# Five feed-forward layers on one core: up and down chunks interleaved, and up chunks as seven products

## The chip, the cores and the metric

The kernel runs on one core of a Trainium2 chip. The metric is the device time of one execution in microseconds; the kernel before has a median of 2759.59 us over three executions (2759.25 to 2760.49).

## What is computed

A block with token mixers and a cross-attention, followed by layers of a second kind, on 512 tokens of width 1024 in float32. Five times in it stands a feed-forward layer with a hidden width of 2816 (22 tiles of 128). They are called FFN 0 to FFN 4 here; FFN 0 has a convolution of width 3 on its gate, the others are plain:

```
def conv_ffn(n, w_up, conv_w, conv_b, w_down):      # FFN 0
    u, g = jnp.split(n @ w_up, 2, axis=-1)
    gc = sum(gp[:, j:j + S] * conv_w[j] for j in range(CONV_WIDTH)) + conv_b
    return (jax.nn.silu(gc) * u) @ w_down

def swiglu(x, w_gate, w_up, w_down):                # FFN 1 to 4
    return (jax.nn.silu(x @ w_gate) * (x @ w_up)) @ w_down
```

Before each stands an RMS norm, whose gain is folded into the operand x and whose factor 1/rms (`rstd`, one number per token) multiplies the products behind the matmuls. Between FFN 0 and FFN 1 there are two norms in a row (`renorm`).

## The kernel before

**Chunks.** All weights come as one stream of chunks of 128x2048 float32 (1 MB). SP loads each into one of two `stage` slots; ACT rounds it into `w_hi` (fp32r, `split_hi`, L508), DVE writes the rest `w_lo = stage - w_hi` (`split_lo`, L1002), and PE multiplies hi*hi, hi*lo and lo*hi (`products`, L1995 to L1997). `stage`, `w_hi` and `w_lo` have two slots each, so the split of chunk c+2 can start only when PE is done with chunk c, and PE starts chunk c+2 only when its `w_lo` is written (`lo_ready`). A slot of `stage` is loaded anew when its `w_lo` is written.

**A chunk on PE.** A gate or up chunk of eight products gives two hidden tiles of 128x512: 16 weight tiles by 3, so 48 matmuls of 128x512. A gate chunk of seven products (`seven_products`) gives the same two tiles with seven block products in place of eight, on half the tokens each: 7 x 4 x 3 = 84 matmuls of 128x256. For it DVE forms four sums of weight blocks (`gate_sums`, four operations of 128x512 into `s_f`, L1023 to L1028), which are split too (ACT `s_hi`, L517; DVE `s_lo`, L1012), and once per FFN sums of token blocks (`token_sums`, sixteen operations of 128x256 into `t_f`, L1066 to L1071, split into `t_hi` and `t_lo`). The block products are put together by DVE (`gate_early`, `gate_evac`). Gate chunks 4 to 10 of FFN 0 and 2 to 10 of the others are of this kind, 43 in all; all up chunks are of eight products.

**An FFN.** Eleven steps `it`, each with a gate chunk and an up chunk. They stand in three parts of 4, 4 and 3 steps; behind each part four down chunks add into the residual `h`. A chunk's results go from PSUM into `gate_b` or `up_b` (DVE, times `rstd`: L1051, L1059, L1140), ACT applies silu (L579; in FFN 0 behind the convolution, six DVE operations L1126 to L1130), POOL multiplies both (L1873), ACT and DVE split the product into `f_hi` (L561) and `f_lo` (L1150), and the down chunks read it. PSUM is used four banks at a time, in turn.

**Start of an FFN.** PE works on gate chunk 0 while POOL ends the sum of squares; then a matmul with ones (`stat`, L2035), ACT's square root (L531), and DVE's reciprocal (L1080; between FFN 0 and 1 L2040, L843 and L1619) give `rstd`, without which nothing of the FFN leaves PSUM. PE goes on with up chunk 0 meanwhile. The order on DVE is written out by hand (`ffn` in the block of DVE); the place that matters most here is

```
                        gate_evac(i, it)
                        if it + 1 < end:
                            gate_lo(i, it + 1)
```

with the token sums behind it, at step 0 for FFN 1 to 4 and at steps 0 and 1, two groups each, for FFN 0.

Of the kernel before, what the change touches and what calls it, by code (L numbers as in the profile page):

```python
# [51 lines left out]
PARTS = [("a", 0, 4), ("b", 4, 4), ("c", 8, 3)]  # L52
SEVEN_FROM = [4, 2, 2, 2, 2]
NONE_OF = FT // 2


def _down_name(i, part):

    return f"down{i}" if part == "c" else f"down{i}{part}"
# [2795 lines left out]
```

## Time and profile before

| | us |
|---|---|
| median of three executions | 2759.59 |
| the profiled execution | 2758.85 |
| its span, first to last instruction | 2757.0 |
| PE busy | 2736.3 (99%) |
| DVE busy | 1827.6 (66%) |
| ACT busy | 963.3 (35%) |
| POOL busy | 530.6 (19%) |
| DMA engines, mean share in the queue of the weights | 27.5% |

Times are from one profiled execution; a row of a timeline begins with the start and the duration of an instruction. Matmuls overlap, so what one costs is the distance between starts, not its duration. Where a row groups several instructions (x2), the duration is from the start of the first to the end of the last.

### The profile page before, as it was taken

The numbers are of one execution on the slowest core, as the hardware profiler recorded it, in microseconds if no ns is written. First come the engines' busy times: TensorE is split into PE (matmuls) and PEld (weight loads), VectorE is DVE, ScalarE is ACT, GpSimd is POOL, SyncE is SP. The second block draws the span as 40 slices with busy tenths as digits, with TensorE's granted clock in tenths as the row PEclk, the third lists the DMA queues.
The fourth block names the chain that finished last, engine by engine and source line by source line (L and its number), as shares of the span: only waits on it lengthen the run. The fifth ranks groups of instructions, "written<-read, shape, count | busy, mean of one in ns | idle before, by whom it ended". The sixth has DMA issues, their size and how long they took to land.

```text
span 2757.0 us, 35919 instructions
## 1 busy us (share of the span) xinstructions
PE 2736.3 (99%) x14384; PEld 2340.8 (85%) x14384; DVE 1827.6 (66%) x2088; ACT 963.3 (35%) x1122; POOL 530.6 (19%) x364
## 2 busy tenths in 40 slices
PE   9999999999999999999999999999999999999999
PEld 7978889878888888988778889888898888888987
DVE  5778766558586885756575857568475665684754
ACT  4433533443232442323363423234232322242322
POOL 0124014041010452002223200023000142510100
PEclk9999999999999999999999999999999999999999
DMA  4212034223222323232302222322323233222232
GB/s 169 90 62 80 31 107 138 92 77 103 96 96 104 108 91 103 96 107 99 108 31 77 92 99 101 104 98 105 107 92 107 93 107 106 92 94 105 92 107 92
DMA packets 39748, 266.02 MB, mean 96 GB/s; under 512 B 4528, under 2 KB 5808, under 8 KB 8240
## 3 DMA queue, kind: packets, MB, share of 16 engines
q1 hardware_dynamic: 38016, 259.02, 27.5%
q10 hardware_dynamic: 1584, 4.87, 0.5%
q8 instruction: 113, 1.85, 0.3%
q14 instruction: 35, 0.29, 0.0%
HBM read 261.77 MB, written 2.10 MB: 96 GB/s over the span
## 4 chain that ended last, share of the span: by engine, by line
PE 95%; DVE 2%; ACT 1%; issue 1%; POOL 1%; DVEq 0%; POOLq 0%; ACTq 0%
PE ps L1995 30%; PE ps L1997 29%; PE ps L1996 29%; PE ps L2202 1%; DVE w_lo L1002 1%; PE ps L2268 1%; PE ps L2299 1%; ACT w_hi L508 1%; PE ps L2590 1%; PE ps L2562 1%; PE ps L2224 1%; PE ps L2282 0%; PE ps L2574 0%; PE ps L2035 0%; POOL up_b L1857 0%
## 5 line engine op out<-in xcount | busy, mean ns | idle before, releaser
L508 ACT ACTIVATE w_hi<-stage 128x2048 fp32r<-128x2048 f32 x241 | 443.5, 1840 | 1323.3 <-PE ps L1997 1321.1
L1995 PE MATMUL ps<-x_hi,w_hi 128*128 128x512 f32 (+1 forms) x2056 | 775.0, 377 | 0.0
L1996 PE MATMUL ps<-x_lo,w_hi 128*128 128x512 f32 (+1 forms) x2056 | 764.8, 372 | 0.0
L1997 PE MATMUL ps<-x_hi,w_lo 128*128 128x512 f32 (+1 forms) x2056 | 764.2, 372 | 0.0
L1002 DVE TENSOR_TENSOR w_lo<-stage,w_hi 128x2048 fp32r<-128x2048 f32 x241 | 580.8, 2410 | 103.1 <-ACT w_hi L508 103.1
L1995 PEld LDWEIGHTS ps<-x_hi,w_hi 128*128 128x128 f32 x2056 | 388.0, 189 | 69.6 <-issue 4.1
L1996 PEld LDWEIGHTS ps<-x_lo,w_hi 128*128 128x128 f32 x2056 | 388.2, 189 | 69.1 <-issue 3.9
L1997 PEld LDWEIGHTS ps<-x_hi,w_lo 128*128 128x128 f32 x2056 | 387.7, 189 | 68.0
L1873 POOL TENSOR_TENSOR up_b<-up_b,gate_b 128x512 f32<-128x512 f32 x110 | 132.1, 1222 | 1405.0 <-DVE up_b L1140 1405.0
L1995 PE MATMUL ps<-f_hi,w_hi 128*128 128x512 f32 x880 | 343.0, 390 | 2.2 <-DVE f_lo L1150 2.2
L1996 PE MATMUL ps<-f_lo,w_hi 128*128 128x512 f32 x880 | 342.5, 389 | 0.0
L1997 PE MATMUL ps<-f_hi,w_lo 128*128 128x512 f32 x880 | 342.3, 389 | 0.0
L1140 DVE TENSOR_TENSOR up_b<-ps,rstd 128x512 f32<-128x512 f32 x110 | 70.8, 686 | 198.6 <-PE ps L1997 198.5
L1995 PEld LDWEIGHTS ps<-f_hi,w_hi 128*128 128x128 f32 x880 | 165.2, 188 | 38.4 <-DVE f_lo L1150 4.3
L1997 PEld LDWEIGHTS ps<-f_hi,w_lo 128*128 128x128 f32 x880 | 165.2, 188 | 34.5
L1996 PEld LDWEIGHTS ps<-f_lo,w_hi 128*128 128x128 f32 x880 | 165.2, 188 | 34.1
L1164 DVE SCALAR_TENSOR_TENSOR h<-ps,h 128x512 f32<-128x512 f32 x80 | 51.5, 686 | 201.0 <-PE ps L1997 201.0
L1851 POOL TENSOR_TENSOR ssum<-ssum,sq 128x512 f32<-128x512 f32 x64 | 146.4, 2287 | 5.0
L1995 PE MATMUL ps<-t_hi,s_hi 128*128 128x256 f32 x516 | 146.0, 283 | 0.0
L1996 PE MATMUL ps<-t_lo,s_hi 128*128 128x256 f32 x516 | 146.0, 283 | 0.0
L1997 PE MATMUL ps<-t_hi,s_lo 128*128 128x256 f32 x516 | 146.0, 283 | 0.0
L1849 POOL TENSOR_TENSOR sq<-h 128x512 f32 x64 | 77.9, 1217 | 269.5 <-DVE h L1093 263.6
(441 smaller groups left out, 4102.6 us busy)
## 6 DMA issues: line engine op xcount, KB each, us to landing
stage<-in_stream SPq DMA_DIRECT2D x242, 1024.0 KB, 4.8
h<-in_x ACTq DMA_DIRECT2D x2, 1024.0 KB, 5.2
out_x<-h SPq DMA_DIRECT2D x8, 256.0 KB, 2.1
h<-in_x SPq DMA_DIRECT2D x6, 256.0 KB, 3.7
mem_raw<-in_mem ACTq DMA_DIRECT2D x1, 1024.0 KB, 4.7
stage<-in_stream SPq DMA_DIRECT2D x6, 128.0 KB, 4.5
h<-in_x SPq DMA_DIRECT2D x1, 512.0 KB, 5.3
mask_f<-in_constants ACTq DMA_DIRECT2D x1, 448.0 KB, 6.1
```

The costliest lines, as they stand in the source:

```text
L508: act.activation(w_hi[slot][:, 0:width], stage[slot][:, 0:width], ACT.Copy).then_inc(hi_ready, 1)
L1002: dve.tensor_tensor(w_lo[slot][:, 0:width], stage[slot][:, 0:width], w_hi[slot][:, 0:width].bitcast(F32), ALU.subtract).then_inc(lo_ready, 1)
L1140: dve.tensor_tensor(up_b[:, e, :], ps[:, (t + 2 + e) % 4, :], rstd[:, :], ALU.mult).then_inc(acc_evac, 1)
L1164: dve.scalar_tensor_tensor(h[:, m, :], ps[:, (t + m) % 4, :], scale, h[:, m, :], ALU.mult, ALU.add).then_inc(acc_evac, 1)
L1849: pool.tensor_tensor(sq[:, :], row(h, m), row(h, m), ALU.mult).then_inc(sq_ready, 1)
L1851: pool.tensor_tensor(ssum[:, :], ssum[:, :], sq[:, :], ALU.add).then_inc(ss_ready, 1)
L1873: pool.tensor_tensor(up_b[:, e, :], up_b[:, e, :], gate_b[:, e, 1:1 + S], ALU.mult).then_inc(prod_ready, 1)
L1995: pe.matmul(out_ap, wh, xh, start=first, stop=False)
L1996: pe.matmul(out_ap, wh, xl, start=False, stop=False)
L1997: return pe.matmul(out_ap, wl, xh, start=False, stop=last)
L2202: mm = pe.matmul(ps[:, bank, b * P:(b + 1) * P], lhs, rhs, start=True, stop=True)
L2224: mm = pe.matmul(ps[:, 5 + 2 * e, :], QQ[e][:, 0, b * P:(b + 1) * P], A[e][:, b, :], start=(b == 0), stop=(b == BLK - 1))
```

## The change

The parts a, b and c are gone. Each FFN has an order of positions p (`ORDER`): gate 0, up 0, gate 1, up 1, gate 2, up 2, down 0, gate 3, up 3, down 1 and so on to gate 10, up 10, then a tail of four down chunks. One of the eight down chunks in between covers four hidden tiles and one half of the outputs (16 weight tiles, 48 matmuls of 128x512, four banks); the tail covers the last six hidden tiles, as part c did. Even positions use the upper, odd ones the lower part of PSUM, so that PE may begin a chunk when the one two positions ahead of it is out of PSUM.

In FFN 1 to 4 the up chunks 2 to 9 are computed with seven products too, and in FFN 0 gate chunk 3 is: 76 chunks in place of 43. `s_f`, `s_hi` and `s_lo` are still there once; a gate chunk now begins with the products that read the sums (`s_used`), and an up chunk ends with them. The block products are put together in five DVE operations behind the chunk's end (`evacuated`), over wider operands, and silu, the product, `f_hi` and `f_lo` take both tiles in one instruction, except at the last step. The tail's chunks are split over 1536 columns where they hold no more.

The core of the diff (the block of DVE first):

```
-PARTS = [("a", 0, 4), ("b", 4, 4), ("c", 8, 3)]
-SEVEN_FROM = [4, 2, 2, 2, 2]
-NONE_OF = FT // 2
...
+def _order():
+
+    out = []
+    for it in range(STEPS):
+        out += [("gate", it), ("up", it)]
+        if 2 <= it < STEPS - 1:
+            out.append(("down", it - 2))
...
+SEVENS = [{"gate": range(3, STEPS), "up": range(0)}] + 4 * [{"gate": range(2, STEPS), "up": range(2, STEPS - 1)}]
...
+        def two_banks(p):
+
+            return 6 if p % 2 == 0 else 0
+
+        def four_banks(p):
+
+            return 4 * (p % 2 == 0)
...
-        T_GROUPS = {i: {0: [0, 1], 1: [2, 3]} if i == 0 else {0: [0, 1, 2, 3]} for i in range(5)}
-        T_ROUND_AT = {i: 1 if i == 0 else 0 for i in range(5)}
+        T_SUMS = [{0: [0, 1], 2: [2, 3]}] + 4 * [{0: [0, 1, 2, 3]}]
+        T_ROUND = [3, 1, 1, 1, 1]
...
+                if kind == "gate":
+                    act.wait_ge(chunk_done, c - 1)
+                elif (i, p - 1) in S_FIRST:
+                    act.wait_ge(s_used, S_FIRST[i, p - 1] + 1)
                 act.activation(s_hi[:, :], s_f[:, :], ACT.Copy).then_inc(s_rounded, 1)
...
+                if kind == "gate":
+                    split_hi((c, 0), SINGLES)
...
+                dve.wait_ge(first_copied, n + 1)
+                dve.tensor_tensor(blocks[:, 0:2, :], product(2, adjacent), free(first, 0, twice_dims), ALU.add).then_inc(blocks_sum, 1)
...
-                dve.scalar_tensor_tensor(t_f[:, T1, j, :], b11, gain[0], t_f[:, T3, j, :], ALU.mult, ALU.subtract).then_inc(t_sum, 1)
-                dve.scalar_tensor_tensor(t_f[:, T3, j, :], b22, gain[1], t_f[:, T3, j, :], ALU.mult, ALU.subtract).then_inc(t_sum, 1)
+                dve.scalar_tensor_tensor(t_f[:, T1, j, :], b12, gain[0], t_f[:, T3, j, :], ALU.mult, ALU.subtract).then_inc(t_sum, 1)
                 dve.wait_ge(t_sum, done + 1)
-                dve.scalar_tensor_tensor(t_f[:, T2, j, :], b22, gain[1], t_f[:, T1, j, :], ALU.mult, ALU.add).then_inc(t_sum, 1)
-                dve.wait_ge(t_sum, done + 3)
+                dve.scalar_tensor_tensor(t_f[:, T2, j, :], b22, gain[1], t_f[:, T1, j, :], ALU.mult, ALU.subtract).then_inc(t_sum, 1)
+                dve.wait_ge(t_sum, done + 2)
+                dve.tensor_tensor(t_f[:, T3, j, :], t_f[:, T2, j, :], t_f[:, T3, j, :], ALU.subtract).then_inc(t_sum, 1)
                 dve.scalar_tensor_tensor(t_f[:, T4, j, :], b21, gain[1], t_f[:, T2, j, :], ALU.mult, ALU.subtract).then_inc(t_sum, 1)
...
-                for part, base, count in PARTS:
-                    end = base + count
-                    for it in range(base, end):
-                        c, t = gate_chunk(i, it)
-                        gate_evac(i, it)
-                        if it + 1 < end:
-                            gate_lo(i, it + 1)
...
+                for p, (kind, it) in enumerate(ORDER):
+                    c, t = chunk_at(i, p)
+                    f, k = FT * i + 2 * it, 2 * it % 8
+                    dve.wait_ge(chunk_done, c + 1)
+                    if kind == "down":
+                        b, m = four_banks(p), 4 * (it % 2)
...
+                        dve.scalar_tensor_tensor(h[:, m:m + 4, :], ps[:, b:b + 4, :], scale, h[:, m:m + 4, :], ALU.mult, ALU.add).then_inc(acc_evac, 4)
+                    elif kind == "gate":
+                        evacuated(i, p, gate_b[:, :, 1:1 + S])
...
-                        for j in T_GROUPS[i].get(it, []):
+                            dve.wait_ge(f_ready, past(f))
+                            convolved(it)
+                        for j in T_SUMS[i].get(p, []):
                             token_sums(i, j)
...
+                            dve.wait_ge(f_hi_ready, f + e + 1)
+                            dve.tensor_tensor(f_lo[:, k + e, :], up_b[:, e, :], f_hi[:, k + e, :].bitcast(F32), ALU.subtract).then_inc(f_ready, 1)
+                    if kind_at(i, p + 2) == ("up", True):
+                        weight_sums(i, p + 2)
+                    ffn_lo(i, p + 2)
+                    if p == T_ROUND[i]:
+                        token_lo(i, 0)
+                        token_lo(i, 1)
+                    if p == T_ROUND[i] + 1:
+                        token_lo(i, 2)
+                        token_lo(i, 3)
+                    if kind_at(i, p + 3) == ("gate", True):
+                        weight_sums(i, p + 3)
+                    if kind == "up" and it < STEPS - 1:
+                        dve.wait_ge(f_hi_ready, f + 2)
+                        dve.tensor_tensor(f_lo[:, k:k + 2, :], up_b[:, :, :], f_hi[:, k:k + 2, :].bitcast(F32), ALU.subtract).then_inc(f_ready, 2)
...
+                def with_sums():
+                    pe.wait_ge(s_ready, n + 1)
+                    product(6, summed(S2), token_sum(T2))
+                    product(7, summed(S3), token_sum(T3))
+                    product(5, summed(S1), token_sum(T1))
+                    return product(3, summed(S4), tokens(1, 1))
+
+                clear(i, p)
+                pe.wait_ge(t_ready, 4 * (i + 1))
+                if kind == "gate":
+                    with_sums().then_inc(s_used, 1)
                 product(1, single(0, 0), tokens(0, 0))
-                product(2, single(1, 0), tokens(1, 0)).then_inc(seven_done, 1)
-                pe.wait_ge(s_ready, n + 1)
-                pe.wait_ge(t_ready, 4 * (i + 1))
-                product(6, summed(S2), token_sum(T2)).then_inc(seven_done, 1)
-                product(7, summed(S3), token_sum(T3)).then_inc(seven_done, 1)
-                product(5, summed(S1), token_sum(T1)).then_inc(seven_done, 1)
-                product(3, summed(S4), tokens(1, 1))
-                product(4, single(1, 1), token_sum(T4)).then_inc(chunk_done, 1)
+                product(2, single(1, 0), tokens(1, 0)).then_inc(first_done, 1)
+                mm = product(4, single(1, 1), token_sum(T4))
+                if kind == "up":
+                    mm = with_sums()
+                mm.then_inc(chunk_done, 1)
...
+                for p, (kind, it) in enumerate(ORDER):
+                    c, t = chunk_at(i, p)
+                    if kind == "down":
+                        clear(i, p)
+                        for k in range(4):
+                            pe.wait_ge(f_ready, past(FT * i + 4 * (it // 2) + k + 1))
+                            for m in range(4):
+                                mm = products(ps[:, four_banks(p) + m, :], w_at(c, (4 * k + m) * P, P),
+                                              (f_hi[:, 4 * (it // 2) % 8 + k, :], f_lo[:, 4 * (it // 2) % 8 + k, :]), k == 0, k == 3)
                         mm.then_inc(chunk_done, 1)
```

On DVE, the order of a step p is now: results of chunk p, then the token sums (position 0; FFN 0: 0 and 2), then the sums and splits of the weights of chunk p+2, then weight sums of a gate chunk at p+3, then `f_lo`.

DVE at the start of FFN 2, from the reciprocal on. Before (`w_lo_57` is the slot that gate chunk 1 uses):

```order
L1080 RECIPROCAL rstd<-ssum 128x512
L1051 TENSOR_TENSOR gate_b<-ps,rstd 128x512 x2
L1002 TENSOR_TENSOR w_lo_57<-stage_53,w_hi_55 128x2048
L1066 SCALAR_TENSOR_TENSOR t_f<-h,par,t_f 128x256
L1067 SCALAR_TENSOR_TENSOR t_f<-h,par,t_f 128x256
L1069 SCALAR_TENSOR_TENSOR t_f<-h,par,t_f 128x256
L1071 SCALAR_TENSOR_TENSOR t_f<-h,par,t_f 128x256
```

And in the change:

```order
L1104 RECIPROCAL rstd<-ssum 128x512
L1065 TENSOR_TENSOR gate_b<-ps,rstd 128x2x512
L1090 SCALAR_TENSOR_TENSOR t_f<-h,par,t_f 128x256
L1092 SCALAR_TENSOR_TENSOR t_f<-h,par,t_f 128x256
L1094 TENSOR_TENSOR t_f<-t_f 128x256
L1095 SCALAR_TENSOR_TENSOR t_f<-h,par,t_f 128x256
...
L1024 TENSOR_TENSOR w_lo_57<-stage_53,w_hi_55 128x2048
L1065 TENSOR_TENSOR up_b<-ps,rstd 128x1024
```

The split of gate chunk 1 stood ahead of the sixteen token sums and now stands behind them (the four rows of `t_f` come four times in both; of the change three times four are left out).

DVE in FFN 2, from the end of an up chunk of seven products to the end of the down chunk behind it, in the change:

```order
L1083 TENSOR_TENSOR up_b<-blocks,rstd 128x1024
L1037 TENSOR_TENSOR s_lo<-s_f,s_hi 128x2048
L1024 TENSOR_TENSOR w_lo_56<-stage_52,w_hi_54 128x1536
L1194 TENSOR_TENSOR f_lo<-up_b,f_hi 128x1024
L1159 SCALAR_TENSOR_TENSOR h<-ps,h 128x2048
L1050 TENSOR_TENSOR s_f<-stage_53 128x512
L1051 TENSOR_TENSOR s_f<-stage_53 128x512
L1053 TENSOR_TENSOR s_f<-s_f,stage_53 128x512
L1055 TENSOR_TENSOR s_f<-stage_53,s_f 128x512
L1024 TENSOR_TENSOR w_lo_57<-stage_53,w_hi_55 128x1536
L1037 TENSOR_TENSOR s_lo<-s_f,s_hi 128x2048
```

Each chunk of seven products brings four `s_f`, one `s_lo` and one `w_lo` of 1536 columns, and this now happens for gate and up in each group of gate, up and down.

DVE at the end of an FFN, behind the results of the last gate chunk, in the change:

```order
L1024 TENSOR_TENSOR w_lo_57<-stage_53,w_hi_55 128x1536
L1177 TENSOR_TENSOR up_b<-ps,rstd 128x512 x2
L1180 TENSOR_TENSOR f_lo<-up_b,f_hi 128x512 x2
L1024 TENSOR_TENSOR w_lo_56<-stage_52,w_hi_54 128x1536
```

Before, a `w_lo` of 2048 columns stood between `up_b` and `f_lo` there.

## Rows read from the trace of the kernel before

**Rows 1.** The page, parts 1 and 2:
```profile
PE 2736.3 (99%) x14384; PEld 2340.8 (85%) x14384; DVE 1827.6 (66%) x2088; ACT 963.3 (35%) x1122; POOL 530.6 (19%) x364
...
PEclk9999999999999999999999999999999999999999
```

**Rows 2.** Timeline of PE, two chunks of FFN 0 (start, duration, instruction):
```profile
756.55 0.28 PE L1995 MATMUL ps<-x_hi,w_hi 128*128 128x256 f32 x1
...
766.62 0.40 PE L1995 MATMUL ps<-x_hi,w_hi 128*128 128x512 f32 x1
...
777.53 0.28 PE L1995 MATMUL ps<-x_hi,w_hi 128*128 128x256 f32 x1
```

**Rows 3.** Timeline of PE, start of FFN 2:
```profile
1528.39 0.79 PE L1995 MATMUL ps<-x_hi,w_hi 128*128 128x512 f32 x1
...
1539.68 0.39 PE L1995 MATMUL ps<-x_hi,w_hi 128*128 128x512 f32 x1
```

**Rows 4.** Timeline of DVE, start of FFN 2:
```profile
1529.71 3.35 DVE L1080 RECIPROCAL rstd<-ssum 128x512 f32<-128x512 f32 x1 [5.05 <-ACT ssum L531]
1533.10 1.29 DVE L1051 TENSOR_TENSOR gate_b<-ps,rstd 128x512 f32<-128x512 f32 x2
1534.30 2.28 DVE L1002 TENSOR_TENSOR w_lo<-stage,w_hi 128x2048 fp32r<-128x2048 f32 x1
1536.50 0.48 DVE L1066 SCALAR_TENSOR_TENSOR t_f<-h,par,t_f 128x256 f32<-128x256 f32 x1
1536.90 0.48 DVE L1067 SCALAR_TENSOR_TENSOR t_f<-h,par,t_f 128x256 f32<-128x256 f32 x1
1537.29 0.48 DVE L1069 SCALAR_TENSOR_TENSOR t_f<-h,par,t_f 128x256 f32<-128x256 f32 x1
1537.81 0.48 DVE L1071 SCALAR_TENSOR_TENSOR t_f<-h,par,t_f 128x256 f32<-128x256 f32 x1
```

**Rows 5.** Timeline of DVE, start of FFN 0:
```profile
623.59 0.54 DVE L1126 TENSOR_SCALAR up_b<-gate_b,par 128x512 f32<-128x512 f32 x1
...
627.65 0.48 DVE L1066 SCALAR_TENSOR_TENSOR t_f<-h,par,t_f 128x256 f32<-128x256 f32 x1
```

**Rows 6.** Timeline of PE, and last row of DVE, start of FFN 1:
```profile
973.20 1.45 PE L2040 MATMUL ps<-up_b,const 128*128 128x512 f32 x2 [2.89 <-POOL up_b L1857]
973.76 1.32 PE L1995 MATMUL ps<-x_hi,w_hi 128*128 128x512 f32 x1
...
986.69 0.39 PE L1995 MATMUL ps<-x_hi,w_hi 128*128 128x512 f32 x1
...
975.40 3.35 DVE L1619 RECIPROCAL rstd<-up_b 128x512 f32<-128x512 f32 x1 [8.55 <-ACT up_b L843]
```

**Rows 7.** Windows: busy us of PE, PEld, DVE, ACT, POOL; granted clock:
```profile
582.00:584.00 2.00, 1.77 (x8) 1.47 (x9) 2.00 (x3) 0.83 (x1) 1.82 (x2) 1.00 0.50 82
975.00:976.00 1.00, 1.00 (x4) 0.81 (x3) 0.60 (x1) 1.00 (x3) 0.82 (x2) 0.50 0.00 0
```

**Rows 8.** Timeline of PE, ACT and DVE, end of FFN 1:
```profile
1290.39 0.39 PE L1997 MATMUL ps<-f_hi,w_lo 128*128 128x512 f32 x1
1291.23 0.50 PE L1995 MATMUL ps<-f_hi,w_hi 128*128 128x512 f32 x1 [0.45 <-DVE f_lo L1150]
...
1287.41 0.63 ACT L561 ACTIVATE f_hi<-up_b 128x512 fp32r<-128x512 f32 x1
...
1287.39 3.19 DVE L1002 TENSOR_TENSOR w_lo<-stage,w_hi 128x2048 fp32r<-128x2048 f32 x1 [0.65 <-ACT w_hi L508]
```

**Rows 9.** Timeline of DVE, work for one chunk of seven products:
```profile
1204.90 0.69 DVE L1023 TENSOR_TENSOR s_f<-stage 128x512 f32<-128x512 f32 x1
...
1213.14 1.76 DVE L1002 TENSOR_TENSOR w_lo<-stage,w_hi 128x1536 fp32r<-128x1536 f32 x1 [0.29 <-ACT w_hi L508]
1214.95 2.29 DVE L1012 TENSOR_TENSOR s_lo<-s_f,s_hi 128x2048 fp32r<-128x2048 f32 x1
```

**Rows 10.** Timeline of PE, a wait of 1.8 us in mem_o:
```profile
582.23 0.50 PE L1995 MATMUL ps<-mo_hi,w_hi 128*128 128x512 f32 x1 [1.65 <-DVE w_lo L1002]
```

More of the change, by code:

```diff
@@ L51 @@
 KP = KT // 2
-PARTS = [("a", 0, 4), ("b", 4, 4), ("c", 8, 3)]
-SEVEN_FROM = [4, 2, 2, 2, 2]
-NONE_OF = FT // 2
-def _down_name(i, part):
-    return f"down{i}" if part == "c" else f"down{i}{part}"
+STEPS = FT // 2
+def _order():
[4 more added lines that the diff above has]
+            out.append(("down", it - 2))
+    return out
+ORDER = _order()
+TILES = {"gate": 2, "up": 2, "down": 4}
+TILE_AT = [sum(TILES[kind] for kind, _ in ORDER[:p]) for p in range(len(ORDER) + 1)]
+LAST_K = 4 * ((STEPS - 3) // 2)
+SEVENS = [{"gate": range(3, STEPS), "up": range(0)}] + 4 * [{"gate": range(2, STEPS), "up": range(2, STEPS - 1)}]
 def _ffn(i):
-    return [phase for part, _, n in PARTS for phase in ((f"up{i}{part}", 2 * n, 4 * n), (_down_name(i, part), 4, 8))]
+    return [(f"up{i}", len(ORDER), TILE_AT[-1]), (f"down{i}", 4, 8)]
 PHASES = [
@@ L538, in step @@
                     for pair in range(2):
-                        split_hi((c0 + 2 + pair, it * 2))
+                        ahead = c0 + 2 + pair, it * 2
+                        split_hi(ahead, 3 * S if name.startswith("down") and it == 0 else CW)
                         for e in range(2):
@@ L1147, in ffn @@
-                        for e in range(2):
-                            k = 2 * it % 8 + e
-                            dve.wait_ge(f_hi_ready, FT * i + 2 * it + e + 1)
-                            dve.tensor_tensor(f_lo[:, k, :], up_b[:, e, :], f_hi[:, k, :].bitcast(F32), ALU.subtract).then_inc(f_ready, 1)
-                        if it + 1 < end and seven(i, it + 1):
-                            gate_early(i, it + 1)
-                        if i == 1 and it == 1:
-                            dve.wait_ge(std_ready, NS0["renorm"] + 1)
-                            dve.reciprocal(sq[:, :], ssum[:, :]).then_inc(rstd_ready, 1)
@@ L1176, in first_piece @@
+                    if i == 1 and (kind, it) == ("gate", 1):
+                        dve.wait_ge(std_ready, NS0["renorm"] + 1)
+                        dve.reciprocal(sq[:, :], ssum[:, :]).then_inc(rstd_ready, 1)
             def first_piece(c, i):
@@ L1877, in ffn @@
                             pool.tensor_scalar(h[:, m, :], h[:, m, :], pc("final_norm", m), None, ALU.mult).then_inc(renormed, 1)
+                    if i == 1 and it == 1:
                         pool.wait_ge(rstd_ready, NS0["renorm"] + 1)
[L1879 to L1880 removed]
+                        for m in range(KT):
                             pool.wait_ge(renormed, KT + m)
@@ L2059, in linear, with clear, eight @@
                     walk(pe, n // 2, step, 1)
-            def eight(c, t, ready):
-                begin(c, t, 2)
+            def clear(i, p):
+                c, t = chunk_at(i, p)
+                pe.wait_ge(lo_ready, c + 1)
+                pe.wait_ge(acc_evac, T0[f"up{i}"] + TILE_AT[p - 1] if p else t - 4)
+            def eight(i, p, ready=None):
+                c, _ = chunk_at(i, p)
+                clear(i, p)
                 for k in range(KT):
```

370 lines of the change are left out of this document (176 added, 194 removed).

## The prediction

> **What bounds the kernel now.** I begin with the page: PE is busy for 2736.3 of 2757.0 us at a full granted clock, DVE for 66% and ACT for 35% [rows 1]. So a gain has to come out of the matmuls, and a loss can come only from a wait of PE that does not exist now. The timeline of PE then gives the price of a chunk. Inside an FFN nothing waits: a chunk of seven products takes 10.07 us from its first matmul to the first of the next (756.55 to 766.62), one of eight 10.91 (766.62 to 777.53) [rows 2]. Per matmul that is 0.120 us at 256 columns and 0.227 us at 512. About 0.03 of the 10.91 belongs to the change from 256 back to 512 columns, which happens equally often in the new order; I take 10.88.
>
> Since PE is full, the question is when the operands of a chunk are ready. The split of chunk c+2 can begin only when chunk c is done, so ACT and DVE have the length of one chunk, some 10 to 11 us, for everything that stands ahead of `w_lo` of chunk c+2. The timeline of DVE at the start of FFN 2 is the one to read for that [rows 4]: DVE gets the statistics late, its reciprocal runs from 1529.71 to 1533.06, and of the up chunk on PE (1528.39 to 1539.68, [rows 3]) six us are left.
>
> **The products.** 76 - 43 = 33 chunks go from eight products to seven: 33 x (10.88 - 10.07) = **-26.7 us**. Cutting the down product differently changes nothing: before 8 chunks of 48 matmuls and 4 of 36 per FFN, after it the same.
>
> The Trainium skill (TensorE: Matmul & The Clock Gate, Back-to-back issue gap) has N/2.4 + 2.5 ns from matmul to matmul, 109 ns at 256 columns and 216 at 512; by that a chunk would save 48 x 0.216 - 84 x 0.109 = 1.2 us and the sum would be 39 us. The trace disagrees on both lengths, and rows decide.
>
> **The start of FFN 2, 3 and 4.** Now the token sums stand ahead of the split of gate chunk 1. On DVE two operations of 512 columns take 1.20 us from start to start (1533.10 to 1534.30) and one of 2048 takes 2.20, so 1024 columns take about 1.13. A token sum of 256 columns takes 0.40, or 0.52 when it waits for the one just before (1537.29 to 1537.81) [rows 4]. The new group of four has two such waits in place of one, and one of its operations reads no parameter and should be the cheapest: 1.76 us, so 7.0 us for four groups. The reciprocal stays where it is, since everything ahead of it does. Then: results of gate 0 from 1533.10 to 1534.23, token sums to 1541.3, `w_lo` (2.28) to 1543.6. PE could begin gate chunk 1 at 1539.68 and waits 3.9 us. The other two start in the same way: 3 x 3.9 = **+11.8 us**. Nothing covers this: the only chunk that PE can run ahead is the one whose operands are waited for.
>
> **The start of FFN 0.** Two groups of token sums (3.5) stand there, but the convolution does too, 4.06 us for its six operations [rows 5]. That is 0.6 more than in FFN 2: 4.5 us. At position 2 the same work stands behind gate chunk 1: 0.3 until DVE sees the end, 1.13 + 4.1 + 3.5 + 2.3 = 11.3 us against an up chunk of 10.88: 0.4. Together **+4.9 us**.
>
> **The start of FFN 1.** PE waits for POOL's sum before the statistics, and its up chunk 0 then runs from 973.76 to 986.69; the reciprocal begins at 975.40 [rows 6]. The distance from reciprocal to the end of `w_lo` is that of FFN 2, 13.9 us, so 989.3, and PE waits 2.7 us. The tail's first chunks are split over 1536 columns now, a quarter less, which should bring ACT's squares and POOL's sum some 0.4 forward (as `w_lo` falls from 2.28 to 1.76, [rows 4, 9]). **+2.3 us**.
>
> **The clock.** Behind the wait that ends at 973.20 the granted clock was 0.50 [rows 7], and the up chunk took 12.93 us where that of FFN 2 takes 11.29 [rows 6, 3]: a loss of 1.6. Behind a wait of 1.65 us in mem_o it stayed at 1.00 [rows 10, 7]. So the price per new wait lies between 0 and 1.6. Four of the new waits (4.5, 3.9 three times) are longer than the one that lowered the clock (2.89 idle, [rows 6]), and I take 1.6 for each: **+6.4 us**. For FFN 1 (2.3) and for the 0.4 in FFN 0 I take nothing.
>
> **The end of an FFN.** The first chunk of the last four down chunks waits for `f_lo`: 1290.39 to 1291.23 is 0.84 in place of 0.23, and the matmul behind starts 0.1 late. On DVE a `w_lo` of 3.19 us from 1287.39 stands ahead of it, while `f_hi` was ready at 1288.04 [rows 8]. The change puts `f_lo` first: the first is then written at about 1288.8 (0.7 for 512 columns), the second, a tile behind it through POOL and ACT, I put a microsecond later. Both are there before 1290.6, when PE comes to the first, and the wait goes: 5 x 0.7 = **-3.5 us**. Next in line is `w_lo` of the second down chunk, 1.76 us behind that, and due 8 us after the first begins.
>
> **The groups in between.** A group of gate, up and down chunk lasts 10.07 + 10.07 + 10.91 = 31.05 us in FFN 1 to 4. DVE's work in it, with 0.6 for 512 columns, 2.2 for 2048 and 1.7 for 1536 [rows 4, 9]: results of a chunk of seven products, 0.7 + 0.5 + 0.7 + 0.7 + 1.2 = 3.8, twice; weight sums 2.5, twice; `s_lo` 2.2 and `w_lo` 1.7, twice; `w_lo` of the down chunk 2.2, its results 2.2, `f_lo` 1.1. That is 25.9 us, plus about 0.9 that DVE loses to POOL's product (`w_lo` 3.19 beside it against 2.28 alone, [rows 8, 4]). It fits, but what counts is each deadline. Behind an up chunk DVE has 10.9 us for 0.3 + 3.8 + 2.2 + 1.7 + 0.9 = 8.9: 2.0 to spare. Behind a gate chunk 10.1 us for 0.3 + 3.8 + 2.2 = 6.3. Behind a down chunk `w_lo` is due after 10.1 and there after 2.2 + 2.5 + 1.7 = 6.4; `s_lo` must wait until PE has read the sums (four of seven products, 5.8 us into the gate chunk), then come ACT's copy, put at DVE's 2.2, and DVE's own 2.2, so it is there at 10.2, and is due only when the first three of the up chunk's products are through, at 14.4. In FFN 0 the convolution stands behind the gate chunk: 0.3 + 3.8 + 4.1 + 2.3 = 10.5 against 10.9. I cost all this at nothing, with DVE's idle time as the cover; in FFN 0 that cover is 0.4 us thick for seven groups, and up to 3 us would be lost if each operation were a tenth slower.
>
> **Sum.** -26.7 + 11.8 + 4.9 + 2.3 + 6.4 - 3.5 = -4.8. From the profiled execution, 2758.85, that gives 2754.0; the median of the runs is 0.7 above it, so **2754.8 us**. About 0.2%, 5.5 us, is what a measurement of this kernel can tell from no change, and the forecast lies just inside.
>
> **Rivals.**
> - The clock stays up behind some or all of the new waits. For it: one wait alone shows a lowered clock, so its length as a bound is uncertain, and part of a lowered stretch can fall into the wait itself, where it costs nothing. Against it: the new waits are longer than that one. All four spared gives 2748.4, two spared 2751.6. Both are faster beyond 0.2%. Chance 0.36.
> - The change does what it says with nothing waiting for it: the split finds room in spite of the token sums, 2759.6 - 26.7 - 3.5 = 2729. The order on DVE and the row of the reciprocal speak against it. Were the matmuls as short as the page quoted above has them, with the waits in place, it would be 12 us below the forecast, at 2742.5; the rows speak against that too. Chance 0.05 for both.
> - Slower: DVE overruns behind each up chunk of seven products. Mechanism: POOL's product of 1024 columns, now one instruction, holds DVE up longer than the 0.9 us of today, or the results that are read across two banks take longer per column. It decides from 2.0 us more on; each 0.5 us beyond costs 8 groups x 4 FFNs x 0.5 = 16 us, so 2771 at 2.5. Against it: POOL's work in sum is the same. Chance 0.09.
> - The same as the forecast, with a fifth lowered clock in FFN 1, the 3 us in FFN 0 and a token sum at 0.46 us: 2754.8 + 1.6 + 3 + 1 = 2760. Chance 0.10.
>
> The forecast itself keeps 0.40; it has a spread of a microsecond or two, so a tenth of the whole lies below 2754.1. The range leaves out the overrun and the cases below 2747: **2746.5 to 2761**. Faster by over 0.2%: 0.36 + 0.05 and a little of the forecast, less what of the first rival stays inside: 0.44. Slower by over 0.2%: the overrun and a part of the last: 0.13. Within: 0.43.
>
> **What would show it.** Right: five rows on PE of a wait for `w_lo` at the second gate chunk of each FFN, 4 us long and 2 to 3 in FFN 1, with a granted clock of 0.50 behind; DVE's `t_f` rows between reciprocal and `w_lo`; 912 records of `t_hi,s_hi` in place of 516; no wait for `f_lo` at an FFN's end. Wrong: a wait for `w_lo` or `s_lo` inside the groups, DVE busy without a gap there, a start of FFN without a wait, or a full clock all along.

## The result and the profile after

The changed kernel has a median of **2765.2 us** (19 executions, 2763.6 to 2766.8) beside 2759.5 for the kernel before (19 executions in the same sessions): ratio 1.0021, 95% interval 1.0014 to 1.0028. It is slower by 5.7 us, where 4.8 less was forecast, and it lies 4 us above the upper end of the range. The profiled execution took 2763.61 us, 4.8 more than the one before.

The page of the changed kernel, parts 1 and 2:

```profile
PE 2720.1 (98%) x15572; PEld 2382.9 (86%) x15572; DVE 2100.4 (76%) x2061; ACT 1006.1 (36%) x1083; POOL 580.6 (21%) x314
...
PEclk9999999999999999999999999999999999999999
```

PE is busy for 16 us less than in [rows 1], the span is 4.8 us longer: some 21 us more of standing still. DVE has 273 us more to do. The page's clock line shows nothing of what follows, since it rounds over 69 us.

The waits of PE by releaser, changed kernel (us in total, times, longest):

```profile
PE ps L2023 <- DVE w_lo L1024: 25.8, 10, 4.6
```

The timeline of PE has these waits one by one; the last bracket is the idle time and what ended it. The order is FFN 0 (two rows), FFN 1 (five rows), FFN 2, 3, 4:

```profile
631.71 0.79 PE L2023 MATMUL ps<-x_hi,w_hi 128*128 128x512 f32 x1 [4.60 <-DVE w_lo L1024]
...
655.63 0.50 PE L2023 MATMUL ps<-x_hi,w_hi 128*128 128x512 f32 x1 [0.53 <-DVE w_lo L1024]
...
977.59 0.70 PE L2068 MATMUL ps<-up_b,const 128*128 128x512 f32 x1 [1.51 <-POOL up_b L1880]
...
993.49 0.80 PE L2023 MATMUL ps<-x_hi,w_hi 128*128 128x512 f32 x1 [3.85 <-DVE w_lo L1024]
...
1029.71 0.39 PE L2023 MATMUL ps<-x_hi,w_hi 128*128 128x256 f32 x1 [1.84 <-DVE w_lo L1024]
...
1042.39 0.50 PE L2023 MATMUL ps<-f_hi,w_hi 128*128 128x512 f32 x1 [0.85 <-DVE w_lo L1024]
...
1054.45 0.39 PE L2023 MATMUL ps<-t_hi,s_hi 128*128 128x256 f32 x1 [0.88 <-DVE w_lo L1024]
...
1550.69 0.80 PE L2023 MATMUL ps<-x_hi,w_hi 128*128 128x512 f32 x1 [3.88 <-DVE w_lo L1024]
...
1903.93 0.50 PE L2023 MATMUL ps<-x_hi,w_hi 128*128 128x512 f32 x1 [3.88 <-DVE w_lo L1024]
...
2431.14 0.79 PE L2023 MATMUL ps<-x_hi,w_hi 128*128 128x512 f32 x1 [3.87 <-DVE w_lo L1024]
```

From the start of the matmul before to the start of the one that waited, each wait costs the bracket and 0.16 us more than usual: 4.76 and 0.69 in FFN 0, 4.04 in FFN 2, 3 and 4. These are the waits that were forecast at 3.9. The three rows from 1029.71 to 1054.45 were not: they stand inside the groups of FFN 1. At the ends of the FFNs there is no wait left (0.54 us before at the end of FFN 0, 0.61 at each of the others, [rows 8]), and inside the groups of FFN 2 to 4 there is none either; FFN 0 has the 0.53 us idle at 655.63 and nothing behind it.

Windows of the changed kernel (busy us of PE, PEld, DVE, ACT, POOL; then the granted clock), each behind one of these waits:

```profile
631.50:634.50 3.00, 2.79 (x7) 2.22 (x8) 3.00 (x3) 0.00 (x0) 1.54 (x1) 0.50 0.51 156
993.50:996.30 2.80, 2.80 (x7) 2.22 (x8) 2.80 (x2) 1.94 (x3) 1.56 (x1) 0.50 0.57 164
1030.60:1033.80 3.20, 3.20 (x17) 3.20 (x17) 3.20 (x2) 1.23 (x1) 3.12 (x2) 0.50 0.84 302
1550.00:1556.00 6.00, 5.30 (x13) 4.15 (x14) 6.00 (x4) 2.69 (x4) 3.89 (x1) 0.50 0.65 199
1904.50:1907.70 3.20, 3.20 (x9) 2.42 (x9) 3.20 (x3) 1.35 (x2) 2.52 (x1) 0.50 0.82 259
2430.10:2436.80 6.70, 5.66 (x13) 4.45 (x14) 6.70 (x4) 3.39 (x5) 3.89 (x1) 0.50 0.63 194
```

The clock was at 0.50, 1.2 GHz, behind each of the new waits of 1.84 us idle and more. In FFN 2 and 4 it stayed there about twice as long as in FFN 3, behind the same wait. What the chunk behind the wait takes over its usual 10.88 us gives the price: 2.7 us in FFN 2, 2.8 in FFN 4, 1.7 in FFN 3, 1.5 in FFN 0 and FFN 1.

DVE and POOL in FFN 1, changed kernel:

```profile
1016.03 3.34 DVE L1197 RECIPROCAL sq<-ssum 128x512 f32<-128x512 f32 x1
...
1020.37 0.67 DVE L1050 TENSOR_TENSOR s_f<-stage 128x512 f32<-128x512 f32 x1
1020.97 2.48 DVE L1051 TENSOR_TENSOR s_f<-stage 128x512 f32<-128x512 f32 x1
1023.37 1.79 DVE L1053 TENSOR_TENSOR s_f<-s_f,stage 128x512 f32<-128x512 f32 x1
1025.19 1.67 DVE L1055 TENSOR_TENSOR s_f<-stage,s_f 128x512 f32<-128x512 f32 x1
1026.79 2.86 DVE L1024 TENSOR_TENSOR w_lo<-stage,w_hi 128x1536 fp32r<-128x1536 f32 x1
1029.58 3.39 DVE L1037 TENSOR_TENSOR s_lo<-s_f,s_hi 128x2048 fp32r<-128x2048 f32 x1
...
1020.62 2.28 POOL L1901 TENSOR_TENSOR up_b<-up_b,gate_b 128x1024 f32<-128x1024 f32 x1 [1.62 <-DVE up_b L1065]
1022.86 17.32 POOL L1910 TENSOR_TENSOR h<-h,sq 128x512 f32<-128x512 f32 x8
```

`s_f` takes 1.7 to 2.5 us in place of 0.69, `w_lo` 2.86 in place of 1.76 [rows 9], `s_lo` 3.39 in place of 2.29, all of them while POOL works off its product and the eight multiplications of `h` for the second norm (L1910). The `w_lo` at 1026.79 is the one for which PE waits until 1029.71.

The place of these multiplications is part of the change, though the account of the change does not name it. Before, they came in two fours, behind the products of steps 2 and 3, and PE waited for nothing there; now all eight stand behind step 1. POOL in FFN 1, kernel before:

```profile
1035.97 6.22 POOL L1882 TENSOR_TENSOR h<-h,sq 128x512 f32<-128x512 f32 x4
...
1054.49 8.14 POOL L1882 TENSOR_TENSOR h<-h,sq 128x512 f32<-128x512 f32 x4
```

FFN by FFN, from the statistics to the end (FFN 1 from the end of FFN 0): FFN 0 is 5.6 us longer than before, FFN 1 1.2 longer, FFN 2, 3 and 4 0.45, 1.4 and 0.35 shorter.

### The profile page after: what moved, and what is told of

It reads as the page before. It is cut to its first block, busy times and chain, and to the rows that moved or that the text cites. A ratio compares the mean times of both kernels' runs of the same rounds, so it can differ in the third digit from the quotient of the medians.

```text
span 2761.8 us, 38306 instructions
## 1 busy us (share of the span) xinstructions
PE 2720.1 (98%) x15572; PEld 2382.9 (86%) x15572; DVE 2100.4 (76%) x2061; ACT 1006.1 (36%) x1083; POOL 580.6 (21%) x314
## 4 chain that ended last, share of the span: by engine, by line
PE 92%; DVE 5%; ACT 1%; issue 1%; POOL 1%; DMA 0%; SPq 0%; DVEq 0%; POOLq 0%; ACTq 0%
PE ps L2023 29%; PE ps L2025 28%; PE ps L2024 28%; DVE w_lo L1024 1%; PE ps L2253 1%; PE ps L2319 1%; PE ps L2350 1%; PE ps L2641 1%; PE ps L2613 1%; PE ps L2275 1%; DVE rstd L1104 0%; DVE t_f L1092 0%; PE ps L2333 0%; ACT w_hi L525 0%; POOL sq L1872 0%
## 5 line engine op out<-in xcount | busy, mean ns | idle before, releaser
L2023 PE MATMUL ps<-x_hi,w_hi 128*128 128x512 f32 (+1 forms) x1792 | 648.5, 362 | 22.9 <-DVE w_lo L1024 22.4
L525 ACT ACTIVATE w_hi<-stage 128x2048 fp32r<-128x2048 f32 (+1 forms) x241 | 419.8, 1742 | 636.7 <-PE ps L2025 634.4
L2025 PE MATMUL ps<-x_hi,w_lo 128*128 128x512 f32 (+1 forms) x1792 | 637.3, 356 | 0.0
L2024 PE MATMUL ps<-x_lo,w_hi 128*128 128x512 f32 (+1 forms) x1792 | 637.3, 356 | 0.0
L1024 DVE TENSOR_TENSOR w_lo<-stage,w_hi 128x2048 fp32r<-128x2048 f32 (+1 forms) x241 | 568.6, 2359 | 42.2 <-ACT w_hi L525 42.2
L1901 POOL TENSOR_TENSOR up_b<-up_b,gate_b 128x1024 f32<-128x1024 f32 x50 | 170.7, 3415 | 1234.8 <-DVE up_b L1083 830.4
L542 ACT ACTIVATE s_hi<-s_f 128x2048 fp32r<-128x2048 f32 x76 | 145.8, 1919 | 342.9 <-PE ps L2025 299.8
L1037 DVE TENSOR_TENSOR s_lo<-s_f,s_hi 128x2048 fp32r<-128x2048 f32 x76 | 184.5, 2427 | 45.5 <-ACT s_hi L542 45.5
L2023 PEld LDWEIGHTS ps<-t_hi,s_hi 128*128 128x128 f32 x912 | 174.9, 192 | 3.0 <-DVE w_lo L1024 1.3
L2024 PEld LDWEIGHTS ps<-t_lo,s_hi 128*128 128x128 f32 x912 | 174.9, 192 | 1.7
```

Source lines behind the costliest of these rows:

```text
L525: act.activation(w_hi[slot][:, 0:width], stage[slot][:, 0:width], ACT.Copy).then_inc(hi_ready, 1)
L542: act.activation(s_hi[:, :], s_f[:, :], ACT.Copy).then_inc(s_rounded, 1)
L1024: dve.tensor_tensor(w_lo[slot][:, 0:width], stage[slot][:, 0:width], w_hi[slot][:, 0:width].bitcast(F32), ALU.subtract).then_inc(lo_ready, 1)
L1037: dve.tensor_tensor(s_lo[:, :], s_f[:, :], s_hi[:, :].bitcast(F32), ALU.subtract).then_inc(s_ready, 1)
L1901: pool.tensor_tensor(up_b[:, :, :], up_b[:, :, :], gate_b[:, :, 1:1 + S], ALU.mult).then_inc(prod_ready, 2)
L2023: pe.matmul(out_ap, wh, xh, start=first, stop=False)
```

## The experiments

Theory A after this reading: the waits at the starts and the clock behind them are the token sums' place in DVE's order, and what FFN 1 loses besides is POOL slowing DVE. Theory B: DVE has too much work of its own, whatever the order and whatever POOL does. All kernels were timed beside the kernel before, which stood at 2759.1 in both sessions.

### The split ahead of the token sums

```
                         evacuated(i, p, gate_b[:, :, 1:1 + S])
+                        early = i == 0 or p == 0
+                        for j in T_SUMS[i].get(p, [])[:0 if i else 0]:
+                            token_sums(i, j)
+                        if early:
+                            ffn_lo(i, p + 2)
                         if i == 0:
                             dve.wait_ge(f_ready, past(f))
                             convolved(it)
-                        for j in T_SUMS[i].get(p, []):
+                        for j in T_SUMS[i].get(p, [])[0 if i else 0:]:
                             token_sums(i, j)
...
-                    ffn_lo(i, p + 2)
+                    if not (kind == "gate" and early):
+                        ffn_lo(i, p + 2)
```

The first new loop is empty here and the second takes all groups. In FFN 0 the split moves ahead of the convolution too, behind every gate chunk.

> The change, with the split w_lo of the next-but-one chunk moved ahead of the token sums at position 0 of every FFN, and ahead of convolution and token sums behind every gate chunk of FFN 0. Theory A (the order on DVE holds PE up at each start of an FFN, and the granted clock falls behind it): the waits of 4.76, 0.69, 4.01, 4.04, 4.04 and 4.03 us go, 21.6 in all, and with them about 10.6 us of low clock; from 2765.2 that is 2733, give or take 3. The waits inside FFN 1 (2.0, 1.0 and 1.0) stay. Theory B (DVE is simply overloaded by the up chunks of seven products, and the order matters little): the waits come back as waits for w_lo or s_lo a chunk or two later, and the time stays over 2750.

Measured: **2738.96** (2737.7 to 2739.4), ratio to before 0.993 (0.991 to 0.994). 26.2 us come back by a change of order alone, so theory B falls; but 6 us fewer than theory A had, outside its 3 either way. The waits for `w_lo` at the five starts and their low clocks are gone; that is 12.1 + 5.4 + 4.0 of waiting and 10.2 of clock, 31.7 us. 26.2 of them show in the time. The rest went into waits behind: four for `t_lo` (3.5 us), and larger ones in FFN 1 (1.6 us more than before the edit, the low clock counted), where the wait of 1.84 us idle has become 2.36 and the one of 0.88 has become 2.54. Timeline of PE in FFN 1, and the first of the waits for `t_lo` in FFN 2 to 4:

```profile
1006.59 0.35 PE L2029 MATMUL ps<-t_hi,s_hi 128*128 128x256 f32 x1 [0.89 <-DVE t_lo L1100]
1017.15 0.39 PE L2029 MATMUL ps<-x_hi,w_hi 128*128 128x256 f32 x1 [0.26 <-DVE w_lo L1024]
1029.86 0.50 PE L2029 MATMUL ps<-f_hi,w_hi 128*128 128x512 f32 x1 [2.36 <-DVE w_lo L1024]
...
1045.18 0.39 PE L2029 MATMUL ps<-t_hi,s_hi 128*128 128x256 f32 x1 [2.54 <-DVE w_lo L1024]
...
1559.96 0.36 PE L2029 MATMUL ps<-t_hi,s_hi 128*128 128x256 f32 x1 [0.67 <-DVE t_lo L1100]
```

DVE's work up to position 4 is the same in both orders, which suggests this reading: as long as PE lost 4 us in front, DVE caught up unseen; now it is DVE that is behind.

### POOL's multiplications in two halves

```
-                    if i == 1 and it == 1:
+                    if i == 1 and it in (2, 3):
                         pool.wait_ge(rstd_ready, NS0["renorm"] + 1)
-                        for m in range(KT):
+                        for m in range(KP * (it - 2), KP * (it - 1)):
```

> The change, with POOL's eight multiplications h*sq of FFN 1 taken in two halves behind the products of steps 2 and 3 (as before the change) in place of all eight behind step 1. Theory A (the three waits inside FFN 1 come from DVE being slowed by POOL there): 2.0, 1.0 and 1.0 us and one stretch of low clock (1.6) go, so 5.6 less than 2765.2: 2759.6. Theory B (the waits come from DVE's own work at the change from eight to seven products, the reciprocal of the second norm among it): they stay, 2765.

Measured: **2765.33**, no change. The three waits are gone, and two new ones of 2.36 and 1.64 us end at the matmuls of 1061.65 and 1095.93, with a low clock behind the first. DVE and POOL there:

```profile
1048.74 2.32 DVE L1194 TENSOR_TENSOR f_lo<-up_b,f_hi 128x1024 fp32r<-128x1024 f32 x1
1055.11 2.29 DVE L1159 SCALAR_TENSOR_TENSOR h<-ps,h 128x2048 f32<-128x2048 f32 x1 [4.05 <-POOL h L1910]
...
1047.17 7.80 POOL L1910 TENSOR_TENSOR h<-h,sq 128x512 f32<-128x512 f32 x4
```

The results of the down chunk are added to `h`, and must wait for POOL's half; all else on DVE is queued behind. The edit misses its aim: it takes the contention at up chunk 2 away and puts a dependence in its place. The time is the one that theory B gave, but not for its reason, since the three waits went; it leaves the theories undecided.

### Both edits

> Both edits together. Theory A: the two are independent, 2733 - 5.6 = 2727.4, give or take 3; PE waits nowhere in an FFN but for POOL's sum at the start of FFN 1. Theory B: over 2750.

Measured: **2737.1** (2736.6 to 2737.3). Only 1.9 us below the first edit, where theory A gave 2727.4, 9.7 less than measured; the reason is the one just seen: DVE stands for 4.06 us behind POOL's half at 1040 too.

### Both edits, and up chunks of FFN 1 to 4 of eight products

```
-SEVENS = [...] + 4 * [{"gate": range(2, STEPS), "up": range(2, STEPS - 1)}]
+SEVENS = [...] + 4 * [{"gate": range(2, STEPS), "up": range(0)}]
```

> Both edits, and the 32 up chunks of FFN 1 to 4 with eight products again. The price of a chunk of seven products is 10.07 us against 10.88, so 32 x 0.81 = 26 us more than with both edits alone: 2753.4 by theory A. By theory B the up chunks of seven products bring waits with them, and taking them back costs less than 15 us.

Measured: **2755.3** (2755.0 to 2755.8), 18.2 more than with sevens, where theory A expected 26 and theory B less than 15; it lies between them. FFN 3 lost 6.39 us = 8 x 0.80, the price that the forecast took from [rows 2]. FFN 1 lost nothing: it took 343.9 us with sevens and 343.4 without, from the statistics to the end. There the up chunks of seven products gain 6.4 us on PE and lose it to waiting.

### POOL's multiplications left out

```
-pool.tensor_tensor(h[:, m, :], h[:, m, :], sq[:, :], ALU.mult).then_inc(renormed, 1)
+pool.tensor_tensor(h[:, m, 0:1], h[:, m, 0:1], sq[:, 0:1], ALU.mult).then_inc(renormed, 1)
```

All eight are cut to one column of 512, so the kernel leaves out nearly all of this work.

> The changed kernel, with POOL's eight multiplications of h by the second norm's factor, between FFN 0 and 1, cut to one column of 512 each (the rest of h is left unmultiplied), everything else as it is. Theory A: beside them DVE's s_f, s_lo and w_lo of FFN 1 take up to 2.6 times as long (s_f 1.7 to 2.5 us in place of 0.69), and that makes PE's waits of 2.00, 1.01 and 1.04 us at 1027.6, 1041.3 and 1053.2 and the low clock behind the first (1.7): 2765.2 - 5.7 = 2759.5. Rival B: it is the work that the change adds to DVE (four s_f and an s_lo per up chunk) with the reciprocal of 3.3 us in the same place; then the waits stay, at most 1 us shorter: 2763.5 or more.

Measured: **2759.56** (2757.1 to 2760.3), 5.6 below the changed kernel. DVE and POOL in FFN 1:

```profile
1017.35 3.34 DVE L1197 RECIPROCAL sq<-ssum 128x512 f32<-128x512 f32 x1
...
1021.68 0.67 DVE L1050 TENSOR_TENSOR s_f<-stage 128x512 f32<-128x512 f32 x1
1022.28 2.49 DVE L1051 TENSOR_TENSOR s_f<-stage 128x512 f32<-128x512 f32 x1
1024.69 0.68 DVE L1053 TENSOR_TENSOR s_f<-s_f,stage 128x512 f32<-128x512 f32 x1
1025.40 0.69 DVE L1055 TENSOR_TENSOR s_f<-stage,s_f 128x512 f32<-128x512 f32 x1
1026.01 1.75 DVE L1024 TENSOR_TENSOR w_lo<-stage,w_hi 128x1536 fp32r<-128x1536 f32 x1
...
1021.94 2.28 POOL L1901 TENSOR_TENSOR up_b<-up_b,gate_b 128x1024 f32<-128x1024 f32 x1 [3.08 <-DVE up_b L1065]
```

Only the `s_f` beside POOL's product is still long (2.49, that is 1.8 more than its 0.69). The reciprocal is where it was, and all three waits are gone:

```profile
PE ps L2023 <- DVE w_lo L1024: 22.2, 7, 4.6
```

So the 5.7 us in FFN 1 are not there without POOL's multiplications, with DVE's own work and its order untouched, and rival B falls. This does not say that the added work is harmless: the next run takes part of it away beside the same multiplications, and the waits go too. It takes both at the same time.

### Up chunks 2 and 3 of FFN 1 of eight products

The first edit, and

```
-SEVENS = [...] + 4 * [{"gate": range(2, STEPS), "up": range(2, STEPS - 1)}]
+SEVENS = [...] + [{"gate": range(2, STEPS), "up": range(4, STEPS - 1)}] + 3 * [{"gate": range(2, STEPS), "up": range(2, STEPS - 1)}]
```

> The first of the moved splits (w_lo ahead of the token sums and of the convolution, 2738.96 us), and in FFN 1 up chunks 2 and 3 of eight products again. Theory A: the time that FFN 1 loses inside its groups is DVE being late beside POOL's eight multiplications of h (18.9 us from 1015.45) and products, in steps 2 and 3 alone. An up chunk of eight products spares DVE the four s_f, s_lo and three of the block additions, about 7 us each, so the waits of 2.52 and 2.70 us at 1027.2 and 1042.3 and the low clock behind (1.7) go, while two chunks cost 0.81 more each: 2738.96 - 6.9 + 1.6 = 2733.7. Rival B: DVE has too little time in FFN 1 whatever POOL does, or the waits only move to where POOL's work then stands: 2738.96 + 1.6 and up, 2740 or more.

Measured: **2733.05** (2733.0 to 2733.5). As expected by A (2733.7). Two chunks cost 0.8 more each and give back 7.5 us, since DVE has room beside POOL. No lowered clock is left in any FFN.

### The last two t_lo earlier, the wait for w_lo later

The edit before, and

```
                 if kind == "gate":
+                    if i and p == T_ROUND[i] + 3:
+                        token_lo(i, 2)
+                        token_lo(i, 3)
                     split_lo((c, 0), SINGLES)
...
-                    if p == T_ROUND[i] + 1:
+                    if i == 0 and p == T_ROUND[i] + 1:
                         token_lo(i, 2)
                         token_lo(i, 3)
...
                 if kind == "gate":
                     with_sums().then_inc(s_used, 1)
+                    pe.wait_ge(lo_ready, c + 1)
```

(the wait for `lo_ready` ahead of such a chunk, in `clear`, is gone).

> As the kernel with up chunks 2 and 3 of FFN 1 of eight products, and at position 4 of FFN 1 to 4 the last two t_lo stand between s_lo and w_lo, while PE waits for the w_lo of a seven-product gate chunk only behind the four products that read the weight sums. Theory A: at position 4 PE waits for t_lo alone (0.83 us in FFN 2, 3 and 4, 1.05 in FFN 1), which then comes 1.7 us sooner, and w_lo is due 5.8 us later than before: 2733.7 - 3 x 0.83 - 1.05 = 2730.2. Rival B: another operand of that chunk is late next (s_lo or the results of chunk 2), so less than half of the 3.5 us comes back: 2732 or more. The difference between the two kernels counts, whatever the first one takes.

Measured: **2729.05** (2728.9 to 2730.1), 4.0 less than without, ratio to before 0.989 (0.9875 to 0.9905). It is the best version of the study, 30 us under the kernel before and 36 under the changed one. Of the waits of PE by releaser, those in an FFN:

```profile
PE ps L2077 <- POOL up_b L1889: 1.5, 1, 1.5
...
PE ps L2032 <- DVE s_lo L1037: 0.8, 1, 0.8
```

Only these two are left in the five FFNs, both in FFN 1: the 1.5 us for POOL's sum and 0.8 for `s_lo` at 1039.4. The expectation was 2730.2, and rival B's 2732 or more is out. The two parts of the edit were not tried apart.

### Three of four groups of token sums ahead of the split

The kernel of 2733.05, with three groups of `token_sums` ahead of `ffn_lo` at position 0 of FFN 2, 3 and 4:

```
-                        for j in T_SUMS[i].get(p, [])[:0 if i else 0]:
+                        for j in T_SUMS[i].get(p, [])[:3 if i > 1 else 0]:
                             token_sums(i, j)
                         if early:
                             ffn_lo(i, p + 2)
...
-                        for j in T_SUMS[i].get(p, [])[0 if i else 0:]:
+                        for j in T_SUMS[i].get(p, [])[3 if i > 1 else 0:]:
                             token_sums(i, j)
```

> As the kernel with up chunks 2 and 3 of FFN 1 of eight products (forecast 2733.7), but in FFN 2, 3 and 4 three of the four groups of token sums stand ahead of the split of gate chunk 1 again, so that w_lo is written 5.3 us later than there and 1.76 us sooner than in the changed kernel, where PE waited 4.04. Both theories: PE waits 4.04 - 1.76 = 2.3 us for w_lo in each of the three, and the 0.83 us that it waits for t_lo at position 4 goes: + 3 x 1.45 = 4.4. Theory A: a wait of 2.3 us is enough to lower the clock (2.0 was, in FFN 1 of the changed kernel), at 1.6 to 1.7 us each: + 4.4 + 5.0 = + 9.4 over the kernel without. Rival B: behind this wait the clock stays up, as behind 1.65 us in mem_o: + 4.4.

Measured: **2739.44** (2738.9 to 2741.0), 6.4 more. The first of PE's three waits (the others are at 1883.53 and 2409.01) and the windows behind all three:

```profile
1534.63 0.50 PE L2029 MATMUL ps<-x_hi,w_hi 128*128 128x512 f32 x1 [2.11 <-DVE w_lo L1024]
```

```profile
1535.00:1540.00 5.00, 5.00 (x24) 4.12 (x23) 4.96 (x6) 3.62 (x4) 2.35 (x1) 1.00 0.57 210
1885.10:1888.30 3.20, 3.20 (x9) 2.55 (x8) 3.20 (x3) 3.02 (x4) 1.75 (x1) 0.50 0.75 297
2409.00:2414.00 5.00, 4.99 (x22) 4.15 (x23) 4.93 (x7) 3.24 (x4) 1.97 (x1) 1.00 0.58 210
```

The waits come out at 2.11 us idle, 2.27 from matmul to matmul, as computed. The clock fell behind one of the three in the profiled execution. So neither side was right about it: 3 x 1.44 + 1.7 = 6.0 against 6.4 measured.

## Why the prediction was wrong

The sum was -4.8; the profiled executions differ by +4.8. Term by term:

| term | forecast | measured | from |
|---|---|---|---|
| 33 chunks of seven products | -26.7 | -26.4 | 0.80 each in FFN 3 (both edits, with and without) |
| start of FFN 2, 3, 4 | +11.8 | +12.1 | 3 x 4.04 |
| start of FFN 0 | +4.9 | +5.4 | 4.76 and 0.69 |
| start of FFN 1 | +2.3 | +2.6 | 4.01 + 1.67 now, 3.05 before |
| low clock there | +6.4 | +8.7 | 1.5, 2.7, 1.7, 2.8; one in FFN 1 as before |
| ends of the FFNs | -3.5 | -3.0 | 0.54 and 4 x 0.61 |
| inside the groups | 0 | +5.7 | 2.00 + 1.01 + 1.04 and a low clock of 1.7 |
| sum | -4.8 | +5.1 | 0.3 more than the two spans differ by |

**The step that failed** is the one that put the groups in between at nothing. The prediction summed DVE's work from rows taken in quiet places and added 0.9 us for POOL's product. That held in FFN 0 and in FFN 2 to 4, where no wait came up inside the groups, even with 0.4 us to spare in FFN 0. It did not hold for FFN 1, which it treated as one of four equal ones. There POOL has sixteen more operations on `h`; the change brings eight of them together behind step 1 and puts the up chunks' new work (four `s_f` and an `s_lo`) beside them. What was put at nothing measured 5.7 us: waits of 2.00, 1.01 and 1.04 and a low clock of 1.7. The multiplications left out gave 5.6 of it back, with DVE's own work untouched. Of the rivals, the overrun of DVE beside POOL had this mechanism, but priced it in all groups of four FFNs at 16 us per half microsecond, and gave it 0.09; it did not look for the one place where POOL has more to do.

**The second** is the size of the clock term. 1.6 us was the price of the one lowered stretch in the trace of before [rows 6, 7]. Behind the waits of 3.9 us it was 1.7 once and 2.7 or 2.8 twice. A stretch at 0.50 costs half of what of it lies outside the wait: in FFN 2 PE worked from 1550.69 to 1556 at 0.50, 5.3 us or a little more, and lost 2.7; in FFN 3 it was 3.4 us, for 1.7. That the clock would fall behind all four waits was right; the first rival, by which it is spared, met no case among them. With the two corrections, +5.7 and +2.3, and 1.9 from small ones, the forecast would have been at 2764.7.

**Luck** had a part in the start of FFN 1, +2.3 forecast and +2.6 measured. The wait for `w_lo` was 4.01 in place of 2.7: the prediction let PE reach gate chunk 1 only at the end of an up chunk that the low clock had stretched to 12.93 us [rows 6], and in the changed kernel that chunk took 11.3 us at full clock, behind a wait of 1.51 us idle in place of 2.89. Against that, POOL's sum was waited for 1.38 us less, in place of 0.4. The clock of FFN 1 came out at nothing as forecast, but because one low stretch of 1.6 us went and another of 1.5 came behind the longer wait. (Two small slips in the working: 989.3 less 986.69 is 2.6, and a tenth more in FFN 0 would be over 4 us for seven groups and not 3; neither moves the forecast by more than 0.1.) The formula that the prediction quotes from the Trainium skill (TensorE: Matmul & The Clock Gate, Back-to-back issue gap) is given there for an isolated matmul and not for a stream; nothing in the sum used it.

**What was right**: the price of a chunk, the order on DVE as the cause of every wait at a start, their length within 0.15 us in FFN 2 to 4, the two waits of FFN 0, and that the ends would wait no more. That the order made the waits at the starts is shown by the first experiment: with the split ahead of the token sums they are gone, and the change is worth 20 us; with FFN 1 spared and `t_lo` moved, 30.

How POOL slows DVE can be read off the rows. POOL's product of 1024 columns takes 2.28 us when it comes first and 3.89 when it comes behind an operation of DVE, in the changed kernel (DVE, then POOL):

```profile
1048.63 2.29 DVE L1037 TENSOR_TENSOR s_lo<-s_f,s_hi 128x2048 fp32r<-128x2048 f32 x1
1050.83 3.56 DVE L1024 TENSOR_TENSOR w_lo<-stage,w_hi 128x1536 fp32r<-128x1536 f32 x1
...
1048.88 3.89 POOL L1901 TENSOR_TENSOR up_b<-up_b,gate_b 128x1024 f32<-128x1024 f32 x1 [8.70 <-DVE up_b L1083]
```

`s_lo` keeps its 2.29 and ends at 1050.92; POOL ends 1.85 us later, at 1052.77; `w_lo`, 1.75 alone, ends 1.62 us after that. So the two take turns, about an instruction each. `s_f`, 0.69, takes 1.79 between two multiplications of 512 columns. The additions that read PSUM do not slow down beside the same eight multiplications, in the changed kernel (DVE, then POOL):

```profile
1035.11 0.68 DVE L1075 TENSOR_TENSOR blocks<-ps,ssum 128x512 f32<-128x512 f32 x1
...
1036.28 0.69 DVE L1079 TENSOR_TENSOR blocks<-ps,blocks 128x512 f32<-128x512 f32 x1
...
1030.89 9.30 POOL L1910 TENSOR_TENSOR h<-h,sq 128x512 f32<-128x512 f32 x4
```

The Trainium skill (SBUF — State Buffer, SBUF: two separate sides) states that a DVE operation with two inputs in SBUF and a GpSimd operation that reads SBUF take a shared pair of ports in turn, for a whole instruction each; the trace agrees, the rows on PSUM included. Up to the end of the `w_lo` that PE waited for, up chunk 2 loses 1.8 + 1.1 + 1.0 us on three `s_f` and 1.1 on `w_lo`, 5.0 in all, and its `s_lo` behind that 1.1 more; the prediction had 2.0 to spare behind an up chunk.

The length of a low stretch does not belong to its FFN. With the multiplications left out, the wait before gate chunk 1 of FFN 2 is 3.87 us idle and ends at 1545.88, the clock is still full for 1.3 us of work behind it, and then down for half as long as in the changed kernel:

```profile
1545.90:1547.20 1.30, 1.30 (x6) 1.08 (x7) 1.30 (x2) 1.30 (x3) 0.07 (x1) 1.00 0.40 69
1547.30:1550.60 3.30, 3.30 (x10) 2.52 (x9) 3.30 (x2) 0.50 (x1) 3.30 (x1) 0.50 0.90 318
```

Even the wait of the kernel before, 2.89 us idle, seems to lower it only sometimes: 24 of its 36 executions beside the experiments have a mean clock of 0.999 and a median of 2759.35, 12 have 1.000 and 2757.6. The 1.8 us between them is about the price of one such stretch; that it is this one is not shown, since only one execution was traced.

Left open: what decides whether the clock falls and for how long, at equal waits. Not tried: POOL's eight multiplications in the changed kernel at their old place without the dependence of the down chunk on them, and up chunk 3 of FFN 1 alone as seven products in the best version.

## What to carry to other kernels

Where one engine is full and another feeds it just in time, look at the order of the feeder at each start: work that is due later (here token sums, due some 20 us later) must not stand ahead of the operand that is due next. Putting it right was worth 26 us, nearly all that the change gained on PE. And when layers look alike, search each for work of its own (here the second norm on POOL) before one is costed for all; a shared engine's extra work costs its neighbour most where the change has just put more. After a wait is taken away, look for what the waiting had hidden: here the `t_lo` of position 4 and DVE's backlog in FFN 1.

## What the hardware showed that was not expected

- The granted clock can fall to 0.50 behind a wait as short as 1.84 us idle (FFN 1), and stayed at 1.00 behind two of three waits of 2.11 us and behind 1.65 in mem_o [rows 7, 10].
- The loss behind equal waits of 3.88 us was 1.7 us in FFN 3, 2.7 in FFN 2 and 2.8 in FFN 4; in another kernel the same wait of FFN 2 (3.87) left the clock down for 3.3 us of work in place of 5.3.
- Beside POOL's operations on two tiles, a DVE operation of 0.69 us took up to 2.49, 3.6 times as long; before, the largest such loss that the forecast had used was 3.19 for 2.28.
